# Narrow passes of a feature-major fp32 block: weight tiles that start at other bytes, and one ring slot read backwards

## The chip, the cores and the metric

One core of a Trainium2 chip runs the whole kernel. The metric is the device time of one execution in microseconds, as a median over several executions; lower is better.

## What is computed

The reference is one residual block over 256 tokens of width 2048, all in float32:

```python
h = rms_norm(x, ln_pre_mix)
proj = h @ w_in                                   # 2048 -> 7680 columns: u, v, q, k, v, two gates
y_a = gmlp_branch(u, v_sg, ...) @ w_a_out
y_b = swa_branch(q, k, v, rel_bias, sinks) @ w_b_out
mix = (gate_a * y_a + gate_b * y_b) @ w_o
x = x + rms_norm(mix, ln_post_mix)
h2 = rms_norm(x, ln_pre_ffn)
x = x + rms_norm(conv_ffn(h2, w_up, conv_w, w_down), ln_post_ffn)   # w_up: 2048 -> 16384, w_down: 8192 -> 2048
```

Each weight matrix is read once, and each product has only 256 rows, one per token.

## The kernel before

**Split numbers.** Every float32 operand of a large product is split into a high part (rounded to the type that TensorE takes at full rate) and a low part (the rest). A product is then three products: high by high, high by low, low by high. ScalarE rounds the high part of the weights (`w_hi`, line 453), VectorE subtracts it to get the low part (`w_lo`, line 861).

**Two ways to multiply.** In the token-major stages (the first projection, `w_o`, `w_down`) the weights are the moving operand: 128x512 passes at lines 1634, 1584, 1777 and 1597. In the feature-major stages the weights are the stationary operand, so that a result stands with its features on the partitions. These stages are q/k/v, u, the gates, `w_a_out`/`w_b_out` (called Y here) and `w_up`. A pass there loads a 128x128 tile of weights and streams activations from `actT`, which holds for each of 16 k-tiles 256 columns of high parts and then 256 of low parts:

- a **wide pass** (`by_hi`, line 1493) loads a tile of `w_hi` and streams all 512 columns, high and low activations;
- a **narrow pass** (`by_lo`, line 1497) loads a tile of `w_lo` and streams the 256 columns of high activations.

**Ring slots.** The weights of a stage come in halves of 1024 columns, numbered h = 0 to 7 in each turn. Half h stands in slot h % 4 of `w_hi` and of `w_lo`. A half gives 8 wide and 8 narrow passes, each with its own 128x128 tile, 512 bytes per partition. `w_hi` slots lie 4096 bytes apart, `w_lo` slots 4608 bytes, `actT` k-tiles 2048 bytes; in the built program the starts of all three are equal modulo 512 bytes. In `w_lo` the data of the feature-major stages begin 8 bytes behind the slot's start:

```python
w_lo_padded = sb("w_lo", [P, RING, HALF + P], F32R)
w_lo = w_lo_padded[:, :, 0:HALF]
w_lo_shifted = [w_lo_padded[:, slot, 2:2 + HALF] for slot in range(RING)]
```

`w_lo_shifted` is written by `split` of VectorE and read by `by_lo`; all other stages use `w_lo`, which begins at the slot's start. Among these is `half_a` (lines 1508 and 1513), which runs the first turn of `w_up`: the same wide and narrow passes, with the narrow ones from `w_lo`.

**The order on TensorE.** `group_turn` runs one turn of 8 halves as four `pair_a`: the pair (0, 1) wide and then narrow, the pair (2, 3) narrow and then wide (`lo_first`), and the same for (4, 5) and (6, 7). So TensorE sees runs of 32 narrow passes (slots 0, 1, 2, 3, 8 passes each) between runs of 32 wide ones (slots 2, 3, 0, 1). In the four turns of Y no pair is `lo_first`, and the runs have 16 passes (slots 0, 1 or 2, 3). 48 turns of 64 wide and 64 narrow passes make 3072 of each. Between some pairs small products of the attention stand.

The loads of weights from memory, ScalarE's rounding and VectorE's subtraction run ahead of TensorE by the ring's four slots; they wait for `half_used`, which TensorE raises once per half.

Of the kernel before, what the change touches and what calls it, by code (L numbers as in the profile page):

```python
# [12 lines left out]
P = 128  # L13
S = 256
# [21 lines left out]
HALF = UNIT // 2  # L36
RAW = 4
RING = 4
# [24 lines left out]
def block_program(nc, x, x_t, pre_gains, w_in, ln_v_g, ln_v_b, w_spatial, b_spatial, rel_bias, sinks, w_a_out, w_b_out,  # L63
# [10 lines left out]
    with ExitStack() as ctx:  # L74
        def sb(name, shape, dt=F32):
            return ctx.enter_context(nc.sbuf_tensor(name, shape, dt))
# [6 lines left out]
        w_hi = sb("w_hi", [P, RING, HALF], F32R)  # L83
        w_lo_padded = sb("w_lo", [P, RING, HALF + P], F32R)
        w_lo = w_lo_padded[:, :, 0:HALF]
        w_lo_shifted = [w_lo_padded[:, slot, 2:2 + HALF] for slot in range(RING)]
        actT = sb("actT", [P, KD, 2, S], F32R)
        xs = sb("xs", [P, RING, 2, S], F32R)
        a_parts = sb("a_parts", [P, 2, 3 * P], F32R)
# [90 lines left out]
        ps = ctx.enter_context(nc.psum_tensor("ps", [P, 8, 512], F32))  # L180
# [1310 lines left out]
        def _(pe):  # L1491
# [2 lines left out]
                                 actT[:, k, :, :].rearrange("p a s -> p (a s)"), start=start, stop=stop)  # L1494

            def by_lo(h, at, k, c, bank, start, stop):
                return pe.matmul(ps[:, bank + c, 0:S], w_lo_shifted[h % RING][:, at:at + P], actT[:, k, 0, :],  # L1497
                                 start=start, stop=stop)

            def half_a(m, h, k0, bank, rows_before):  # L1500

# [39 lines left out]
            def pair_a(m, h0, k0, k_first, k_last, bank, lo_first=False, branch_lo=False):  # L1541
# [14 lines left out]
                def run_lo(signal):  # L1556
                    for h in (h0, h0 + 1):
                        pe.wait_ge(lo_ready, 8 * m + (h + 1))
                        if branch_lo and lo_first:
                            pe.wait_ge(br_lo, h + 1)  # L1560
                        for i in range(4):
                            k = k0 + (h - h0) * 4 + i
                            for c in range(2):
                                ins = by_lo(h, i * GC + c * P, k, c, bank, lo_first and k == k_first,
                                            not lo_first and k == k_last)
                        if signal:
                            ins.then_inc(half_used, 1)
# [356 lines left out]
```

## Time and profile before

| | before |
|---|---|
| median of 3 runs | 1583.93 us (1583.9 to 1583.99) |
| the profiled execution: its own time | 1583.59 us |
| its span, first to last instruction | 1581.8 us |
| TensorE matmul busy | 1572.7 us (99%) |
| TensorE weight load busy | 1360.7 us (86%) |
| VectorE busy | 1260.6 us (80%) |
| ScalarE busy | 827.8 us (52%) |
| wide passes, line 1493 | 3072, 717.6 us |
| narrow passes, line 1497 | 3072, 377.9 us |

Matmuls overlap in the profile, because each one's end is modelled with the time through the array. The length of one (390 ns for a wide pass) is therefore not what it costs: the distance from one start to the next is. A row of the timeline that merges n passes tells it as (its length minus one pass's length) / (n - 1). A row of the grouped view gives nearly the same as busy time over count.

### The profile page before, as it was taken

The numbers are of one execution on the slowest core, as the hardware profiler recorded it, in microseconds if no ns is written. First come the engines' busy times: TensorE is split into PE (matmuls) and PEld (weight loads), VectorE is DVE, ScalarE is ACT, GpSimd is POOL, SyncE is SP. The second block draws the span as 40 slices with busy tenths as digits, with TensorE's granted clock in tenths as the row PEclk, the third lists the DMA queues.
The fourth block names the chain that finished last, engine by engine and source line by source line (L and its number), as shares of the span: only waits on it lengthen the run. The fifth ranks groups of instructions, "written<-read, shape, count | busy, mean of one in ns | idle before, by whom it ended". The sixth has DMA issues, their size and how long they took to land.

```text
span 1581.8 us, 24342 instructions
## 1 busy us (share of the span) xinstructions
PE 1572.7 (99%) x8652; PEld 1360.7 (86%) x8652; DVE 1260.6 (80%) x1836; ACT 827.8 (52%) x1124; POOL 1.9 (0%) x12
## 2 busy tenths in 40 slices
PE   9999999999999999999999999999999999999998
PEld 8888888888888888888888888888888888888886
DVE  6566677677797788777787777877778899989998
ACT  7544544456565654444444444444444575766664
POOL 0000000000000000000000000000000000000000
PEclk9999999999999999999999999999999999999999
DMA  9885455556566465556655666665655555555562
GB/s 371 272 232 189 160 186 168 178 160 209 191 241 218 152 210 188 187 186 203 190 189 187 186 201 191 190 187 186 200 191 191 209 208 206 201 204 195 186 213 107
DMA packets 234946, 313.15 MB, mean 198 GB/s; under 512 B 5360, under 2 KB 209808, under 8 KB 234000
## 3 DMA queue, kind: packets, MB, share of 16 engines
q1 hardware_dynamic: 231056, 306.44, 58.8%
q10 hardware_dynamic: 3840, 6.05, 1.5%
q8 instruction: 32, 0.52, 0.1%
q14 instruction: 18, 0.15, 0.0%
HBM read 309.58 MB, written 2.88 MB: 198 GB/s over the span
## 4 chain that ended last, share of the span: by engine, by line
PE 96%; DVE 4%; issue 0%; ACT 0%; DVEq 0%
PE ps L1493 44%; PE ps L1497 23%; PE ps L1584 15%; PE ps L1777 6%; PE ps L1634 3%; PE ps L1597 1%; DVE actT L1188 1%; DVE w_lo L1188 1%; PE ps L1508 1%; PE ps L1513 0%; DVE arena L1176 0%; PE ps L1723 0%; PE ps L1704 0%; PE ps L1656 0%; PE ps L1716 0%
## 5 line engine op out<-in xcount | busy, mean ns | idle before, releaser
L1493 PE MATMUL ps<-actT,w_hi 128*128 128x512 f32 x3072 | 717.6, 390 | 0.0
L453 ACT ACTIVATE w_hi<-raw 128x1024 fp32r<-128x1024 f32 x420 | 433.1, 1055 | 504.6 <-PE ps L1493 253.7
L861 DVE TENSOR_TENSOR w_lo<-raw,w_hi 128x1024 fp32r<-128x1024 f32 x422 | 506.4, 1224 | 232.3 <-ACT w_hi L453 230.1
L1493 PEld LDWEIGHTS ps<-actT,w_hi 128*128 128x128 f32 x3072 | 568.9, 188 | 114.6 <-issue 0.2
L1497 PEld LDWEIGHTS ps<-actT,w_lo 128*128 128x128 f32 x3072 | 372.4, 188 | 10.3 <-issue 1.7
L1497 PE MATMUL ps<-actT,w_lo 128*128 128x256 f32 x3072 | 377.9, 279 | 0.0
L1584 PE MATMUL ps<-w_hi,xs 128*128 128x512 f32 x832 | 226.6, 389 | 0.0
L1584 PEld LDWEIGHTS ps<-w_hi,xs 128*128 128x128 f32 x832 | 156.1, 188 | 32.4
L1584 PE MATMUL ps<-w_lo,xs 128*128 128x512 f32 x416 | 128.1, 389 | 0.0
L1188 DVE TENSOR_TENSOR w_lo<-raw,w_hi 128x1024 fp32r<-128x1024 f32 x96 | 117.4, 1222 | 0.0
L1378 DVE SCALAR_TENSOR_TENSOR arena<-arena,convw 128x256 f32<-128x256 f32 x256 | 106.8, 480 | 0.0
L712 ACT ACTIVATE w_hi<-raw 128x1024 fp32r<-128x1024 f32 x96 | 100.5, 1046 | 0.0
L1584 PEld LDWEIGHTS ps<-w_lo,xs 128*128 128x128 f32 x416 | 78.1, 188 | 16.3
L1777 PE MATMUL ps<-actT 128*128 128x512 f32 x288 | 81.0, 389 | 0.1
L690 ACT ACTIVATE actT<-raw 128x1024 fp32r<-128x1024 f32 x24 | 25.4, 1060 | 99.0 <-PE ps L1777 99.0
L872 DVE TENSOR_TENSOR arena<-ps,arena 128x512 f32<-128x512 f32 (+1 forms) x106 | 72.6, 685 | 1.5 <-ACT arena L466 1.4
L1777 PE MATMUL ps<-actT,a_parts 128*128 128x512 f32 x216 | 64.7, 390 | 0.0
L1777 PEld LDWEIGHTS ps<-actT 128*128 128x128 f32 x288 | 54.0, 188 | 11.8 <-DVE actT L1188 0.6
L466 ACT ACTIVATE arena<-ps 128x512 f32<-128x512 f32 x106 | 61.4, 579 | 2.8 <-PE ps L1513 1.4
L1188 DVE TENSOR_TENSOR actT<-arena,actT 128x1024 fp32r<-128x1024 f32 (+2 forms) x52 | 59.8, 1161 | 0.0
L710 ACT ACTIVATE xs<-arena 128x256 fp32r<-128x256 f32 x96 | 38.8, 404 | 24.7 <-PE ps L1584 13.8
L1366 DVE TENSOR_TENSOR arena<-arena,rrow 128x512 f32<-128x512 f32 x64 | 44.3, 692 | 6.5
(181 smaller groups left out, 935.4 us busy)
## 6 DMA issues: line engine op xcount, KB each, us to landing
raw<-in_w_up_dram SPq DMA_DIRECT2D x128, 1024.0 KB, 5.7
raw<-in_w_down_dram SPq DMA_DIRECT2D x64, 1024.0 KB, 5.2
raw<-in_w_in_dram SPq DMA_DIRECT2D x58, 1024.0 KB, 5.2
raw<-in_w_o_dram SPq DMA_DIRECT2D x16, 1024.0 KB, 5.3
raw<-in_w_a_out_dram SPq DMA_DIRECT2D x8, 1024.0 KB, 5.3
raw<-in_w_b_out_dram SPq DMA_DIRECT2D x8, 1024.0 KB, 5.2
arena<-in_x_dram SPq DMA_DIRECT2D x1, 2048.0 KB, 16.7
arena<-in_x_dram ACTq DMA_DIRECT2D x2, 1024.0 KB, 6.3
```

The costliest lines, as they stand in the source:

```text
L453: act.activation(w_hi[:, h % RING, :], raw[:, h // 2, h % 2 * HALF:(h % 2 + 1) * HALF], ACT.Copy)\
L466: act.activation(lo_part, ps[:, bank:bank + 2, S:2 * S], ACT.Copy).then_inc(copied, 1)
L712: act.activation(w_hi[:, slot, :], raw[:, unit.slot, j * HALF:(j + 1) * HALF], ACT.Copy).then_inc(hi_ready, 1)
L861: dve.tensor_tensor(lo, raw[:, h // 2, h % 2 * HALF:(h % 2 + 1) * HALF], w_hi[:, h % RING, :].bitcast(F32), ALU.subtract).then_inc(lo_read ...
L872: dve.tensor_tensor(dst, ps[:, bank:bank + 2, 0:S], lo_part, ALU.add).then_inc(summed, 1)
L1188: return dve.tensor_tensor(lo, full, hi.bitcast(F32), ALU.subtract)
L1378: dve.scalar_tensor_tensor(out=dst[:, a, :], in0=src[:, a, i:i + S], scalar=w(i, a), in1=dst[:, a, :], op0=ALU.mult, op1=ALU.add).then_inc ...
L1493: return pe.matmul(ps[:, bank + c, :], w_hi[:, h % RING, at:at + P], actT[:, k, :, :].rearrange("p a s -> p (a s)"), start=start, stop=stop)
L1497: return pe.matmul(ps[:, bank + c, 0:S], w_lo_shifted[h % RING][:, at:at + P], actT[:, k, 0, :], start=start, stop=stop)
L1584: ins = pe.matmul(ps[:, bank + 2 * t + c, :], xpart[:, tokens], wpart[:, slot, c * 512:(c + 1) * 512], start=(first and xpart is x_hi and ...
L1634: ins = pe.matmul(ps[:, 4 + 2 * t + c, :], xpart[:, t * P:(t + 1) * P], wpart[:, slot, c * 512:(c + 1) * 512], start=(k == 0 and xpart is ...
L1777: ins = pe.matmul(ps[:, bank, :], x[x_part], y[y_part], start=(unit.first and alone and x_part + y_part == 0), stop=(unit.last and alone a ...
```

## The change

Three numbers and a direction change. The low parts of the feature-major stages begin 34, 50 and 18 floats (136, 200 and 72 bytes) behind the start of slots 0, 1 and 2; in slot 3 they stay at 2 floats (8 bytes). All four are the old 8 bytes plus a multiple of 64: plus 128, 192, 64 and 0. VectorE writes them there, and the narrow passes load their tiles from there. The narrow passes of slot 3 stream their 256 columns from the last to the first, and write their 256 results from the last to the first, so that each result stands where it stood. No instruction is added, removed or moved on any engine, and no wait changes.

```diff
         w_lo = w_lo_padded[:, :, 0:HALF]
-        w_lo_shifted = [w_lo_padded[:, slot, 2:2 + HALF] for slot in range(RING)]
+        LO_SHIFT = (34, 50, 18, 2)
+        w_lo_shifted = [w_lo_padded[:, slot, shift:shift + HALF] for slot, shift in enumerate(LO_SHIFT)]
+        BACKWARDS = 3
...
             def by_lo(h, at, k, c, bank, start, stop):
-                return pe.matmul(ps[:, bank + c, 0:S], w_lo_shifted[h % RING][:, at:at + P], actT[:, k, 0, :],
-                                 start=start, stop=stop)
+                step = -1 if h % RING == BACKWARDS else 1
+                return pe.matmul(ps[:, bank + c, 0:S][:, ::step], w_lo_shifted[h % RING][:, at:at + P],
+                                 actT[:, k, 0, ::step], start=start, stop=stop)
```

## Rows read from the trace of the kernel before

**Rows 1.** The page: busy time by engine, granted clock in 40 slices, chain that ended last.

```profile
PE 1572.7 (99%) x8652; PEld 1360.7 (86%) x8652; DVE 1260.6 (80%) x1836; ACT 827.8 (52%) x1124; POOL 1.9 (0%) x12
...
PEclk9999999999999999999999999999999999999999
...
PE 96%; DVE 4%; issue 0%; ACT 0%; DVEq 0%
PE ps L1493 44%; PE ps L1497 23%; PE ps L1584 15%; PE ps L1777 6%; PE ps L1634 3%; PE ps L1597 1%; DVE actT L1188 1%; DVE w_lo L1188 1%; PE ps L1508 1%; PE ps L1513 0%; DVE arena L1176 0%; PE ps L1723 0%; PE ps L1704 0%; PE ps L1656 0%; PE ps L1716 0%
```

**Rows 2.** Waits of TensorE: engine line waited for, us, times, longest.

```profile
PE ps L1656 <- DVE rrow L929: 1.2, 1, 1.2
PE ps L1823 <- DVE arena L1294: 0.5, 1, 0.5
PE ps L1525 <- DVE actT L918: 0.4, 1, 0.4
```

**Rows 3.** The page's groups: busy us, mean ns of one, idle before.

```profile
L1493 PE MATMUL ps<-actT,w_hi 128*128 128x512 f32 x3072 | 717.6, 390 | 0.0
...
L861 DVE TENSOR_TENSOR w_lo<-raw,w_hi 128x1024 fp32r<-128x1024 f32 x422 | 506.4, 1224 | 232.3 <-ACT w_hi L453 230.1
L1493 PEld LDWEIGHTS ps<-actT,w_hi 128*128 128x128 f32 x3072 | 568.9, 188 | 114.6 <-issue 0.2
L1497 PEld LDWEIGHTS ps<-actT,w_lo 128*128 128x128 f32 x3072 | 372.4, 188 | 10.3 <-issue 1.7
L1497 PE MATMUL ps<-actT,w_lo 128*128 128x256 f32 x3072 | 377.9, 279 | 0.0
...
L1188 DVE TENSOR_TENSOR w_lo<-raw,w_hi 128x1024 fp32r<-128x1024 f32 x96 | 117.4, 1222 | 0.0
```

**Rows 4.** Timeline of TensorE in two turns of w_up: start us, length us, line.

```profile
704.45 3.87 PE L1497 MATMUL ps<-actT,w_lo 128*128 128x256 f32 x32
708.15 7.44 PE L1493 MATMUL ps<-actT,w_hi 128*128 128x512 f32 x32
715.43 3.87 PE L1497 MATMUL ps<-actT,w_lo 128*128 128x256 f32 x32
719.14 7.45 PE L1493 MATMUL ps<-actT,w_hi 128*128 128x512 f32 x32
```

**Rows 5.** Timeline of TensorE in the first turn of w_up.

```profile
540.64 1.11 PE L1513 MATMUL ps<-actT,w_lo 128*128 128x256 f32 x8
541.59 1.04 PE L1831 MATMUL ps<-ident,arena 128*128 128x128 f32 x8
...
544.31 1.12 PE L1513 MATMUL ps<-actT,w_lo 128*128 128x256 f32 x8
545.26 2.00 PE L1508 MATMUL ps<-actT,w_hi 128*128 128x512 f32 x8
```

**Rows 6.** Two lines of code: duration ns min/median/max, first and last start.

```profile
L1513 PE MATMUL ps<-actT,w_lo x48: 277/283/283, 540.6 to 557.2; 128*128 128x256 f32 x48
...
L1831 PE MATMUL ps<-ident,arena x24: 270/272/273, 535.1 to 548.8; 128*128 128x128 f32 x24
```

**Rows 7.** Timeline of TensorE, five short windows: start and middle of runs.

```profile
540.88 0.88 PE L1513 MATMUL ps<-actT,w_lo 128*128 128x256 f32 x6
...
704.45 0.75 PE L1497 MATMUL ps<-actT,w_lo 128*128 128x256 f32 x5
...
704.80 1.43 PE L1497 MATMUL ps<-actT,w_lo 128*128 128x256 f32 x11
...
708.15 1.55 PE L1493 MATMUL ps<-actT,w_hi 128*128 128x512 f32 x6
...
711.81 2.43 PE L1493 MATMUL ps<-actT,w_hi 128*128 128x512 f32 x10
```

**Rows 8.** Windows, line 1497 alone: busy of PE, of PEld, clock, DMA.

```profile
49.00:337.00 288.00, 99.02 (x784) 95.69 (x784) 1.00 0.62 192
337.00:426.00 89.00, 30.93 (x244) 30.50 (x245) 1.00 0.57 181
...
557.00:1239.00 682.00, 240.32 (x1984) 238.80 (x1984) 1.00 0.61 191
```

**Rows 9.** Windows, all engines: PE, PEld, DVE, ACT, POOL busy.

```profile
557.00:1239.00 682.00, 682.00 (x3974) 602.81 (x3974) 533.42 (x788) 305.55 (x347) 0.00 (x0) 1.00 0.61 191
```

## The prediction

> **What bounds the kernel now.** I read the page first. TensorE is busy for 99% of the span at a granted clock of nine tenths or more in every slice, and the chain that ended last runs through it for 96% [rows 1]. In that chain the wide passes of line 1493 hold 44% and the narrow passes of line 1497 hold 23%. The waits of TensorE come to 2.1 us in three places, none of them at either line [rows 2]. So no engine keeps TensorE waiting in the feature-major stages; what counts there is how fast one pass follows another. VectorE, the busiest of the others, works 533 us of the 682 us of w_up [rows 9]. It could follow a TensorE that is some per cent faster.
>
> The second reading is the distance between starts. The timeline shows a run of 32 narrow passes from 704.45 to 708.15, which is 3.70 / 32 = 115.6 ns each, and then 32 wide ones to 715.43, 227.5 ns each [rows 4]. Columns alone don't give these numbers: a wide pass has twice the columns of a narrow one, so 227.5 - 115.6 = 111.9 ns would be the price of 256 columns, and the narrow pass costs 3.7 ns more than that. Per pass, a tile of 128x128 weights is loaded beside the stream of the pass before, and the load itself is shown as 188 ns long [rows 3].
>
> The third reading is the one on which the forecast turns. The first turn of w_up runs the same narrow pass, with the same two operands, but with tiles that begin at the slot's start (line 1513). Six of them in the middle of a run take (0.88 - 0.283) / 5 = 119.4 ns each [rows 6, 7]. Eleven of line 1497, whose tiles begin 8 bytes further, take (1.43 - 0.279) / 10 = 115.1 ns each [rows 3, 7]. So where a tile begins, relative to the columns that are streamed, moves a narrow pass by 4.3 ns. Over 3072 passes that is 13 us.
>
> The Trainium skill says otherwise (SBUF — State Buffer, Who interferes with whom): TensorE has a read port for the stream and another for the weights, and never waits for anyone. By that rule a start address is free, the two rows should read alike, and this change would be worth 0 us. The trace disagrees, by those 4.3 ns; the rule comes back below as a rival.
>
> **The change part by part.**
>
> *The writes of VectorE.* It subtracts into the slots at another byte. Between the old 8 bytes (line 861, 1224 ns) and none (line 1188, 1222 ns) there is no difference to speak of [rows 3]. Cost 0, covered besides by VectorE's idle time; were the cover gone, 2 ns x 422 would be under 1 us.
>
> *Slots 0, 1 and 2: 2304 of the 3072 narrow passes.* No row has a tile that begins 64, 128 or 192 bytes behind the place where the stream begins, so I bound it. Below: a 128x128 pass from the identity (line 1831) streams half the columns of a narrow one and loads a tile of the same size; eight follow each other at (1.04 - 0.272) / 7 = 109.7 ns [rows 5, 6]. That they do not run at half the narrow pass's distance tells that the load of the tile sets them, and a narrow pass can't do better than its load. From 115.1 to 109.7 is 5.4 ns, times 2304 is 12.4 us gained. Above: the price without any offset, 119.4 ns, which is 4.3 x 2304 = 9.9 us lost.
> Which value? The rows have only one step away from equal starts, and it was a gain. They don't say whether the gain came from those 8 bytes inside a small unit, which all four slots keep, or from distance as such, which grows in three slots. I take half of the way that is left to the load's price: 2.7 ns x 2304 = 6.2 us gained. This is a choice between ends that lie on both sides; it is the weakest number here.
>
> *Changes of place inside a run.* A run doesn't reach its pace at once. The first five narrow passes after wide ones take (0.75 - 0.279) / 4 = 117.8 ns, against 115.1 in the middle; six wide ones after narrow ones take (1.55 - 0.39) / 5 = 232 ns against (2.43 - 0.39) / 9 = 226.7 ns in the middle [rows 3, 7]. TensorE settles again whenever the relation of tile and stream changes. Today slots 0 to 3 have one relation, so a run of 32 settles once. With four relations it settles at three more places, 2 runs in each of 44 turns, and at one more place in each of the 16 runs of 16 in Y: 264 + 16 = 280 places. The price of one is 4 passes x 2.7 ns = 11 ns, so 3.0 us lost. Below, it is 0, if the slots don't differ; above, 8 passes at 2.7 ns, 6.0 us.
>
> *Slot 3 backwards: 768 passes.* No row has a stream that goes backwards, in or out. Both streams keep their bytes; only the sense in which the activations run against the tile's load turns round. Below, the load's price again: 5.4 x 768 = 4.1 us gained. Above, a stream that goes at half its pace would cost a narrow pass what a wide one costs, 227.5 - 115.6 = 112 ns more, and 768 x 112 = 86 us. These ends are far apart; the nearest row is the forward pass itself, which reads the same operands in the same places, and I take 0.
>
> *Sum.* -6.2 + 3.0 + 0 = -3.2 us. The profiled execution took 1583.59 us, so 1580.4; the median of before lies 0.3 us higher, so **1580.7 us** after. All of it is on the path: 784, 244 and 1984 narrow passes lie in the three stretches [rows 8], and TensorE has no slack there.
>
> **The rivals.**
>
> *Nothing moves.* If only the place inside a unit of 64 bytes counts, the 8 bytes that all slots keep are all there is; the three added distances are multiples of 64 and change nothing, and direction may be as idle. For it: the 8 bytes had their effect although they are a small part of a 512-byte tile, and within a run the slots 0, 1, 2 and 3 begin 4608 bytes apart and yet run evenly. Against it: wide passes settle over several passes, so the relation of the two streams over longer distances counts too. The skill's rule above leads to the same place for another reason, and the trace has gone against that reason. Time: 1583.9 us.
>
> *The relation gets worse.* The old offset may be a good place, and others worse. A narrow pass then sits at the price of an unsettled or an aligned one. At 117.8 ns for slots 0 to 2 it is 2.7 x 2304 = 6.2 us lost, with the 3.0 us of settling 9.2, so 1593 us; at 119.4 ns 9.9 + 3.0 = 12.9, so 1597. For it: the unsettled paces of the rows are all slower than the settled ones, narrow and wide, and 8 passes per slot leave little time to settle. Against it: a settled pace was reached from every start that the trace has. Smaller losses belong here too: with the settling's 3.0 us already lost, 0.2 us more make the result slower by over 0.2%.
>
> *Backwards is dear.* Here one thing alone ends on the slower side: the pass of slot 3 pays for reading or writing from last to first. Its place is every fourth stay in a ring slot, 768 passes. It cancels the gain of 3.2 us from 4.2 ns per pass and makes the kernel slower by over 0.2% from 8.4 ns; at half pace the sum is +83 us, so 1667. For it: nothing in this kernel goes that way, so no row vouches for it. Against it: neighbours stay neighbours, and the bytes touched are the same. The skill (Advanced Engine Details and Errata, PSUM Cachelines) asks that every two consecutive elements of an output lie together, in lines of 8 bytes, and says that matmuls slow down otherwise. A backward output keeps its pairs, so by the letter of the rule it is free; no run so far shows it.
>
> **How the numbers follow.** 0.2% of this time is 3.2 us, about what a measurement of this kernel can tell from no change. The forecast case, a gain in the moved slots that outweighs the settling, is the likeliest at 0.45: of its outcomes some stay under 0.2% and most, up to the bound of 12.4 + 4.1 = 16.5 us, are beyond it. Nothing moves: 0.20. A worse relation: 0.28. Backwards dear: 0.07. From these come faster by over 0.2% 0.40 (the forecast case less the part that is too small), same 0.27 (nothing moves, and the small ends of the two cases beside it), slower 0.33. The range must leave out no more than 2 in 10: below, 1571 us takes in all but the last 4 us of the bound; above, 1595 takes in the worse relation up to the unsettled price and a little of the way to the aligned one, and leaves the rest of it and the dear backward pass outside. For the likeliest case alone the range is 1570 to 1583.
>
> **What would show it.** In the profile after, the runs of 32 narrow passes have four stays of 8, and windows over each give a pace per slot. The forecast wants slots 0 to 2 at about 112.4 ns once settled, a slower first pass or two after each change of slot, slot 3 near 115, and wide passes at 226.7 as before. Nothing moved would show all four at 115. A worse relation would show paces from 117 to 120 in slots 0 to 2. A dear backward pass stands out in slot 3 alone. Line 861 should stay at 1224 ns, and the waits of TensorE at 2.1 us. What would make it all wrong: that the pace of wide passes changes because the load of `w_hi` tiles follows the last narrow passes in another relation, which no term here holds; or that a distance of 64 bytes and more has an effect of another size than the two rows of lines 1497 and 1513 span.

## The result and the profile after

| | before | after |
|---|---|---|
| median | 1583.96 us (4 runs) | 1591.26 us (4 runs, 1590.91 to 1591.54) |
| ratio | | 1.0046, 95% interval 1.0034 to 1.0059 |
| profiled execution, span | 1581.8 us | 1589.7 us |

The change made the kernel 7.3 us slower. The prediction said 1580.7 us, faster, with a range from 1571 to 1595. The measured time lies inside the range, but the kernel moved the other way.

The page of the kernel after, busy time by engine, the chain, and the groups that answer to [rows 3] (by_hi stands at line 1495 now, by_lo at 1500, VectorE's subtraction at 863):

```profile
PE 1580.4 (99%) x8652; PEld 1368.7 (86%) x8652; DVE 1260.6 (79%) x1836; ACT 828.0 (52%) x1124; POOL 1.9 (0%) x12
...
PE ps L1495 44%; PE ps L1500 23%; PE ps L1587 15%; PE ps L1780 6%; PE ps L1637 2%; PE ps L1600 1%; DVE actT L1190 1%; DVE w_lo L1190 1%; PE ps L1511 1%; DMA raw<-in_w_in_dram 1%; PE ps L1516 0%; DVE arena L1178 0%; PE ps L1726 0%; PE ps L1707 0%; PE ps L1719 0%
...
L1495 PE MATMUL ps<-actT,w_hi 128*128 128x512 f32 x3072 | 716.6, 390 | 0.0
...
L863 DVE TENSOR_TENSOR w_lo<-raw,w_hi 128x1024 fp32r<-128x1024 f32 x422 | 506.3, 1223 | 239.9 <-ACT w_hi L455 237.7
...
L1500 PEld LDWEIGHTS ps<-actT,w_lo 128*128 128x128 f32 x3072 | 380.2, 188 | 10.8 <-issue 1.7
L1500 PE MATMUL ps<-actT,w_lo 128*128 128x256 f32 x3072 | 386.1, 282 | 0.0
...
L1587 PE MATMUL ps<-w_hi,xs 128*128 128x512 f32 x832 | 226.6, 389 | 0.0
```

The loss stands in one row. The narrow passes went from 377.9 to 386.1 us, 8.2 us more, and the wide ones from 717.6 to 716.6, 1.0 us less; together 7.2 us. VectorE's writes to the new places cost what they did (506.3 against 506.4 us), and the token-major passes kept their 226.6 us; of before the page has:

```profile
L1584 PE MATMUL ps<-w_hi,xs 128*128 128x512 f32 x832 | 226.6, 389 | 0.0
```

The waits of TensorE (engine line waited for, us, times, longest) are those of [rows 2] and one of 0.2 us:

```profile
PE ps L1659 <- DVE rrow L931: 1.2, 1, 1.2
PE ps L1826 <- DVE arena L1296: 0.5, 1, 0.5
PE ps L1528 <- DVE actT L920: 0.4, 1, 0.4
PE ps L1637 <- ACT w_hi L455: 0.2, 1, 0.2
```

So TensorE waits 0.2 us more than it did, and the other 7 us are not waits; its passes follow each other more slowly. The timeline of TensorE shows where. One run of 32 narrow passes in w_up, the run of wide ones behind it, and then windows that take 7 passes of each stay of 8, in slots 0, 1, 2 and 3, and the first ten wide passes:

```profile
708.16 3.96 PE L1500 MATMUL ps<-actT,w_lo 128*128 128x256 f32 x32
711.96 7.43 PE L1495 MATMUL ps<-actT,w_hi 128*128 128x512 f32 x32
...
708.28 0.99 PE L1500 MATMUL ps<-actT,w_lo 128*128 128x256 f32 x7
...
709.23 0.98 PE L1500 MATMUL ps<-actT,w_lo 128*128 128x256 f32 x7
...
710.17 1.00 PE L1500 MATMUL ps<-actT,w_lo 128*128 128x256 f32 x7
...
711.12 1.00 PE L1500 MATMUL ps<-actT,w_lo 128*128 128x256 f32 x7
...
711.96 2.44 PE L1495 MATMUL ps<-actT,w_hi 128*128 128x512 f32 x10
```

The run takes 711.96 - 708.16 = 3.80 us where [rows 4] had 3.70. Slot by slot, (length - 0.28) / 6 gives 118, 117, 120 and 120 ns; no stay is at the 115.1 ns of [rows 7].

A hundredth of a microsecond is coarse for that. The turns of w_up repeat so exactly that the starts can be averaged over 28 of them, which gives each distance to a tenth of a ns. In thirteen of the seventeen kernels below the distances then come out as whole multiples of 0.833 ns, the "units" of the expectations; in all_1, all_10, enter_34_stay_50 and act_8 many don't. This table is worked out from the traces in that way: mean distance from start to start in ns in each stay of 8 passes, and the time of a turn (two runs of 32 narrow and two of 32 wide passes). The places are bytes from the slot's start.

```
kernel             places of slots 0-3      narrow, slot 0    1      2      3    wide, first 8   turn, us
before             8 8 8 8                         116.7  115.6  115.4  115.4          230.0     21.973
after              136 200 72 8, 3 backwards       117.8  117.8  119.9  119.7          227.9     22.147
shifts_only        136 200 72 8                    117.8  117.8  119.9  117.3          227.8     22.107
back_only          8 8 8 8, 3 backwards            116.7  115.6  115.4  118.6          232.2     22.080
all_34             136, all slots                  117.8  117.8  118.2  117.8          230.6     22.133
all_18             72, all slots                   118.6  118.1  118.2  118.3          230.1     22.147
all_50             200, all slots                  118.8  120.0  120.0  119.8          229.8     22.227
all_0              0, all slots                    119.1  120.0  120.0  120.0          230.1     22.227
all_back           8, all slots, all backwards     119.2  119.9  120.0  120.0          228.2     22.200
enter_34_stay_50   136 200 200 200                 117.8  117.6  116.7  116.7          231.3     22.107
all_66             264, all slots                  116.7  115.6  115.4  115.4          230.0     21.973
all_1              4, all slots                    117.8  118.3  118.3  117.8          230.0     22.133
all_4              16, all slots                   118.3  118.3  118.3  118.3          232.0     22.173
all_6              24, all slots                   121.1  121.2  121.5  121.9          227.9     22.307
all_10             40, all slots                   118.3  119.2  119.2  119.0          230.1     22.173
hi_8               8, w_hi at 8 too                116.7  115.6  115.4  115.6          230.5     22.180
act_8              8, actT at 8 too                119.9  119.6  120.7  119.5          232.2     22.547
```

In all rows but the last two the wide passes settle at 226.7 ns. In hi_8 the two narrow runs of a turn differ in their first stay, 116.7 and 117.6 ns; the row shows one. The table holds for w_up. Of the 121 narrow runs of the kernel 71 have 32 passes, 62 of them in w_up; the other 50, in the stages before it, have 16.

### The profile page after: what moved, and what is told of

Same layout as the page of the kernel before. It is cut to its first block, busy times and chain, and to the rows that moved or that the text cites. A ratio compares the mean times of both kernels' runs of the same rounds, so it can differ in the third digit from the quotient of the medians.

```text
span 1589.7 us, 24342 instructions
## 1 busy us (share of the span) xinstructions
PE 1580.4 (99%) x8652; PEld 1368.7 (86%) x8652; DVE 1260.6 (79%) x1836; ACT 828.0 (52%) x1124; POOL 1.9 (0%) x12
## 4 chain that ended last, share of the span: by engine, by line
PE 95%; DVE 4%; DMA 1%; SPq 0%; issue 0%; ACT 0%; DVEq 0%
PE ps L1495 44%; PE ps L1500 23%; PE ps L1587 15%; PE ps L1780 6%; PE ps L1637 2%; PE ps L1600 1%; DVE actT L1190 1%; DVE w_lo L1190 1%; PE ps L1511 1%; DMA raw<-in_w_in_dram 1%; PE ps L1516 0%; DVE arena L1178 0%; PE ps L1726 0%; PE ps L1707 0%; PE ps L1719 0%
## 5 line engine op out<-in xcount | busy, mean ns | idle before, releaser
L1495 PE MATMUL ps<-actT,w_hi 128*128 128x512 f32 x3072 | 716.6, 390 | 0.0
L863 DVE TENSOR_TENSOR w_lo<-raw,w_hi 128x1024 fp32r<-128x1024 f32 x422 | 506.3, 1223 | 239.9 <-ACT w_hi L455 237.7
L1500 PEld LDWEIGHTS ps<-actT,w_lo 128*128 128x128 f32 x3072 | 380.2, 188 | 10.8 <-issue 1.7
L1500 PE MATMUL ps<-actT,w_lo 128*128 128x256 f32 x3072 | 386.1, 282 | 0.0
L1587 PE MATMUL ps<-w_hi,xs 128*128 128x512 f32 x832 | 226.6, 389 | 0.0
L1587 PE MATMUL ps<-w_lo,xs 128*128 128x512 f32 x416 | 128.1, 389 | 0.0
```

Of the source, the lines that this page charges most:

```text
L863: dve.tensor_tensor(lo, raw[:, h // 2, h % 2 * HALF:(h % 2 + 1) * HALF], w_hi[:, h % RING, :].bitcast(F32), ALU.subtract).then_inc(lo_read ...
L1495: return pe.matmul(ps[:, bank + c, :], w_hi[:, h % RING, at:at + P], actT[:, k, :, :].rearrange("p a s -> p (a s)"), start=start, stop=stop)
L1500: return pe.matmul(ps[:, bank + c, 0:S][:, ::step], w_lo_shifted[h % RING][:, at:at + P], actT[:, k, 0, ::step], start=start, stop=stop)
L1587: ins = pe.matmul(ps[:, bank + 2 * t + c, :], xpart[:, tokens], wpart[:, slot, c * 512:(c + 1) * 512], start=(first and xpart is x_hi and ...
```

## The experiments

### The two parts by themselves

From here on the diffs are against the kernel after; the step is -1 where `h % RING in BACKWARDS`. First the places without the direction:

```diff
         LO_SHIFT = (34, 50, 18, 2)
-        BACKWARDS = 3
+        BACKWARDS = ()
```

> The three moved slots as in the change, slot 3 forwards again. Every theory must give back what the trace after shows of slot 3: its stay of 8 narrow passes takes 0.957 us there against 0.923 before. Theory 1 (each offset has a pace of its own): slots 0, 1, 2 stay at about 0.943, 0.943 and 0.959 us per stay, slot 3 returns to 0.923 to 0.93 us; the kernel takes 1588 to 1590 us. Theory 2 (every change of offset costs a settling, whatever the offset): slot 3 still follows a slot with another offset, so its stay remains above 0.94 us; 1590 to 1591 us. Theory 3 (the backward pass is the only loss): 1584 us.

Measured: 1589.15 us, before beside it 1583.80, ratio 1.0033 (1.0021 to 1.0046). So the three places alone lose 5.4 us. The stays of slots 0 to 2 are those of the kernel after, to a tenth of a ns. Slot 3 came back to 117.3 ns, not to 115.4: it follows a slot with another place and pays 1.9 ns x 8 = 15 ns for that. Theories 1 and 2 each have a part of it. Theory 3, by which the backward pass was the only loss, falls.

Then the direction without the places:

```diff
-        LO_SHIFT = (34, 50, 18, 2)
-        BACKWARDS = 3
+        LO_SHIFT = (2, 2, 2, 2)
+        BACKWARDS = (3,)
```

> All four slots at 8 bytes as before, slot 3 backwards. If the backward pass costs by itself, slot 3 takes 0.95 to 0.96 us per stay and slots 0 to 2 stay at 0.923 to 0.934; a part of the 0.034 us per stay comes back in the wide passes that follow, since those after the change settle in 2 passes and not in 5; 1585.5 to 1587.5 us. If it lost only because of its neighbours' offsets, 1584 us. If direction is all of the loss, 1591 us.

Measured: 1587.94 us, ratio 1.0026 (1.0017 to 1.0036). The backward slot alone loses 4.1 us, more than the 1585.5 to 1587.5 that I had for it. The timeline of TensorE, 7 passes of slot 3 and the first ten wide passes behind them:

```profile
709.24 1.00 PE L1500 MATMUL ps<-actT,w_lo 128*128 128x256 f32 x7
...
710.07 2.48 PE L1495 MATMUL ps<-actT,w_hi 128*128 128x512 f32 x10
```

The same window of the wide passes in the kernel before:

```profile
708.15 2.46 PE L1493 MATMUL ps<-actT,w_hi 128*128 128x512 f32 x10
```

The passes themselves cost 118.6 against 115.4 ns, 3.2 x 8 = 26 ns per stay. The wide passes behind them then take (2.48 - 0.39) / 9 = 232.2 ns where (2.46 - 0.39) / 9 = 230.0 is the time of before, so in w_up they lose nearly as much again. In the kernel after, the same window gives (2.44 - 0.39) / 9 = 227.8, and shifts_only has the same in the table. So behind three moved slots the wide passes settle sooner, whichever way slot 3 goes. The grouped views of shifts_only (first two lines) and of back_only:

```profile
L1495 PE MATMUL ps<-actT,w_hi 128*128 128x512 f32 x3072 | 716.2, 390 | 0.0
L1500 PE MATMUL ps<-actT,w_lo 128*128 128x256 f32 x3072 | 384.5, 281 | 0.0
...
L1495 PE MATMUL ps<-actT,w_hi 128*128 128x512 f32 x3072 | 719.0, 391 | 0.0
L1500 PE MATMUL ps<-actT,w_lo 128*128 128x256 f32 x3072 | 380.5, 280 | 0.0
```

Over the whole kernel the backward slot alone costs 2.6 us in the narrow row and 1.4 in the wide one. 5.4 and 4.1 us together are more than the 7.3 us of the whole change for two reasons of about 1 us each. In the wide row, 1.4 us less and 1.4 us more would cancel, and the whole change has 1.0 us less. In the narrow row, 6.6 and 2.6 us would make 9.2, and the whole change has 8.2: slot 3 has a loss in either part alone, and the two don't add up.

### One place in all four slots

```diff
+        LO_SHIFT = (34,) * 4           # all_34; 18, 50, 0 likewise
+        BACKWARDS = ()
```

> All four slots at 136 bytes, all forwards, so no change of offset inside a run. Theory 1 (each offset has its pace): the pace of slot 0 after, 117.8 ns, holds in all four slots and never falls to 115.6; the kernel takes 1589 to 1592 us. Theory 2 (only changes of offset cost): after the first five passes of a run the pace is 115.6 ns, and the kernel takes 1584 us.

> All four slots at 72 bytes, all forwards. Theory 1 (each offset has its pace): 119.9 ns as in slot 2 after, or whatever it settles to with 32 passes at hand, but not 115.6; 1594 to 1598 us. Theory 2 (only changes of offset cost): 1584 us. A third outcome is possible: 72 bytes settles to a pace of its own only after more than 8 passes, so the stays of the second half of a run are faster than the first.

> All four slots at 0 bytes, forwards: tiles and stream begin at equal places modulo 512 bytes. Theory 1 (each offset has its pace) expects the pace of line 1513 of before, 120 ns, in all 3072 passes: 4.4 ns more than at 8 bytes, 1595 to 1597 us. If line 1513 is slow for another reason (runs of 8 only, other semaphores), about 1584 us.

> All four slots at 200 bytes, forwards. Slot 1 after showed 140 units of 0.833 ns (116.7 ns) in six passes in a row behind a slot at 136 bytes. Theory 1 (each offset has its pace): 116.7 ns holds through the run, 1586 to 1588 us. If slot 1 owed its pace to its neighbours, the pace is another, between 117.5 and 120 ns, and 1590 to 1596 us.

| | place, bytes | median, us | ratio to before (95%) |
|---|---|---|---|
| all_34 | 136 | 1590.79 | 1.0044 (1.0028 to 1.0060) |
| all_18 | 72 | 1591.74 | 1.0050 (1.0034 to 1.0066) |
| all_0 | 0 | 1595.05 | 1.0070 (1.0050 to 1.0090) |
| all_50 | 200 | 1594.32 | 1.0065 (1.0045 to 1.0086) |

With no change of place inside a run, none of them comes back to the time of before. Theory 2, by which only changes cost, falls: a place has a pace. At 136 bytes slot 0's 117.8 ns holds in all slots, as expected. At 0 bytes the narrow passes of the whole kernel take on the pace of line 1513, 120.0 ns, so that line's pace needs no other reason than its place. The timeline of TensorE in all_0, one run:

```profile
709.75 4.00 PE L1500 MATMUL ps<-actT,w_lo 128*128 128x256 f32 x32
713.58 7.44 PE L1495 MATMUL ps<-actT,w_hi 128*128 128x512 f32 x32
```

(4.00 - 0.283) / 31 = 119.9 ns. The loads of the narrow tiles are shown 192 ns long in this run, against 188 before. In all_50, at the same 120.0 ns, they are shown 189 ns long. So the length of the load doesn't tell the pace.

But two of the four went against the plain form of theory 1, and against the times that it gave. At 72 bytes the pace is 118.2 ns, not the 119.9 that slot 2 showed in the change. At 200 bytes it is 120.0 ns, not the 116.7 that slot 1 settled to in the change (six distances of 140 units in a row).

### Can one place have two paces?

```diff
+        LO_SHIFT = (34, 50, 50, 50)    # enter_34_stay_50
+        BACKWARDS = ()
```

> Slot 0 at 136 bytes, slots 1, 2 and 3 at 200 bytes, all forwards. At 200 bytes in all slots a narrow pass took 144 units of 0.833 ns; in slot 1 after, behind a slot at 136 bytes, 140 units, six times in a row. If one offset has more than one settled pace and the entry decides, slots 1 to 3 hold 140 units for up to 24 passes and the kernel takes 1588 to 1590 us. If the 140 of slot 1 was a passage on the way to 144, the later stays climb to 144 and the kernel takes 1591 to 1594 us.

Measured: 1590.30 us, ratio 1.0039 (1.0023 to 1.0055), which lies between the times of the two theories, 0.3 us above the first and 0.7 below the second. The pace decides. The timeline of TensorE, 15 passes of slots 2 and 3:

```profile
709.59 1.92 PE L1500 MATMUL ps<-actT,w_lo 128*128 128x256 f32 x15
```

and in all_50, the last 16 passes of a run, at the same place:

```profile
710.88 2.08 PE L1500 MATMUL ps<-actT,w_lo 128*128 128x256 f32 x16
```

(1.92 - 0.28) / 14 = 117 ns against (2.08 - 0.28) / 15 = 120 ns. The same 200 bytes, the same operands, the same engine work: entered from wide passes the run settles at 120.0 ns, entered by way of 8 passes at 136 bytes it settles at a mean of 116.7 and holds that for 23 passes to the run's end. So this place has two settled paces, and what came before decides which.

### Backwards in all four slots

```diff
+        LO_SHIFT = (2,) * 4            # all_back
+        BACKWARDS = (0, 1, 2, 3)
```

> All four slots at 8 bytes, every narrow pass backwards. Slot 3 alone backwards cost 31 units of 0.833 ns per stay of 8 passes against forwards, and the wide passes behind it took 22 to 33 more. If backwards has a pace of its own (142.5 units, 118.7 ns), the kernel takes 1592 to 1595 us. If what cost was the change of direction inside a run, the later stays return to 138 to 139 units and the kernel takes 1584 to 1587 us.

Measured: 1594.33 us, ratio 1.0065 (1.0045 to 1.0086). Backwards has a pace of its own at this place, 120.0 ns against the 115.6 of before, and it doesn't recover in the later stays. A stream at half its pace is excluded: 4.4 ns, not 112. Whether the cost comes from reading backwards, from writing backwards, or from the stream's first column lying 1020 bytes further on, no run here separates. Nor did any run go backwards at another place.

### Where the good place is, and what repeats

```diff
+        LO_SHIFT = (66,) * 4           # all_66; 1, 4, 6, 10 likewise
+        BACKWARDS = ()
```

> All four slots at 264 bytes, 8 plus 256, forwards. If the relation of tile and stream repeats after 256 bytes, the pace is that of 8 bytes, 115.6 ns, and the kernel takes 1584 us. If the place in the whole tile of 512 bytes counts, the pace is another one, between 117 and 120 ns as at 72, 136 and 200 bytes: 1590 to 1595 us.

> All four slots at 4 bytes, forwards. With a straddled small unit as the cause, 4 bytes gives a pace between those of 0 and 8 bytes or equal to that of 8: 115.6 to 120 ns, 1584 to 1595 us. Under 1583 us would show that 8 bytes was not the best place.

> All four slots at 16 bytes, forwards. If the gain of 8 bytes over 0 comes from a tile that straddles a small unit, a whole 16 bytes gives 0's pace back, 120 ns and 1595 us. If it comes from distance, 16 bytes is as good as 8 or better, 1580 to 1585 us.

> All four slots at 24 bytes, 8 plus 16, forwards. If only the place inside 16 bytes counted, 24 would be as 8: 1584 us; the runs at 72, 136 and 200 bytes speak against it. Else a pace between 140 and 144 units, 1589 to 1595 us. A pace under 138 units, below 1583 us, would be a better place than before's.

> All four slots at 40 bytes, 8 plus 32, forwards. With places of 72, 136 and 200 bytes at 142, 141.5 and 144 units, a smooth curve over the distance would give about 140 units, 1587 us; without one, anything from 138 to 144 units, 1583 to 1595 us. Below 1583 us would be a better place than before's.

| | place, bytes | median, us | ratio to before (95%) |
|---|---|---|---|
| all_66 | 264 | 1583.74 | 0.9999 (0.9988 to 1.0010) |
| all_1 | 4 | 1590.85 | 1.0044 (1.0024 to 1.0063) |
| all_4 | 16 | 1592.39 | 1.0052 (1.0029 to 1.0075) |
| all_6 | 24 | 1598.16 | 1.0090 (1.0060 to 1.0119) |
| all_10 | 40 | 1592.63 | 1.0054 (1.0032 to 1.0077) |

The timeline of TensorE in all_66, one run:

```profile
704.41 3.87 PE L1500 MATMUL ps<-actT,w_lo 128*128 128x256 f32 x32
708.11 7.45 PE L1495 MATMUL ps<-actT,w_hi 128*128 128x512 f32 x32
```

This is [rows 4] again, and in the averaged starts each of the 128 distances of a turn agrees with before to about a tenth of a unit. Moving a tile by 256 bytes does nothing, at this one place where it was tried; moving it by 64, 128 or 192 does. And all_6, one run:

```profile
710.93 4.05 PE L1500 MATMUL ps<-actT,w_lo 128*128 128x256 f32 x32
```

24 bytes give (4.05 - 0.285) / 31 = 121.5 ns, worse than no offset at all, although 24 is 8 plus 16. So neither the place within 16 bytes nor the distance orders the paces: 0, 4, 8, 16, 24 and 40 bytes stand at 120.0, 118.3, 115.4, 118.3, 121.5 and 119.2 ns. 16 bytes met neither of its two expectations, and 24 bytes lies above its range. Among the nine places tried, and 264 as 8, 8 is the only fast one, and no version here beats the kernel before.

### Tile or stream?

```diff
-        w_hi = sb("w_hi", [P, RING, HALF], F32R)
+        w_hi_padded = sb("w_hi", [P, RING, HALF + P], F32R)                       # hi_8
+        w_hi = w_hi_padded[:, :, 2:2 + HALF]
...
-        actT = sb("actT", [P, KD, 2, S], F32R)
+        actT_padded = sb("actT", [P, KD * 2 * S + P], F32R)                       # act_8
+        actT = actT_padded[:, 2:2 + KD * 2 * S].rearrange("p (k a s) -> p k a s", k=KD, a=2)
```

Both start from the kernel before, with its 8 bytes in `w_lo`, and these diffs are against it. The padding also sets the slots of `w_hi` 4608 instead of 4096 bytes apart and moves what lies behind; all this is in multiples of 512 bytes, and no run has the padding without the 8 bytes.

> The kernel before, with the high parts begun 8 bytes behind the slot's start too, in all stages. If what the 8 bytes do to a narrow pass comes from the relation of a tile's place and the stream's, the wide passes gain as the narrow ones did, from 272 units (226.7 ns) to about 267 (222 ns): 3072 x 4.4 ns = 13.6 us, 1570 to 1573 us, and possibly the passes of lines 1584, 1777 and 1634 move as well, where w_hi is the stream. If wide passes are set by something else, 1584 us; if 8 bytes cost the stream, slower.

Measured: 1601.61 us, ratio 1.0111 (1.0094 to 1.0128), the largest miss of the study. The grouped view of hi_8 (busy us, mean ns of one, idle before):

```profile
L1494 PE MATMUL ps<-actT,w_hi 128*128 128x512 f32 x3072 | 726.2, 393 | 0.0
...
L1498 PE MATMUL ps<-actT,w_lo 128*128 128x256 f32 x3072 | 378.1, 279 | 0.0
...
L1585 PE MATMUL ps<-w_hi,xs 128*128 128x512 f32 x832 | 232.0, 395 | 0.0
L1585 PE MATMUL ps<-w_lo,xs 128*128 128x512 f32 x416 | 130.0, 393 | 0.0
```

The narrow passes stayed (378.1 against 377.9 us). The wide ones, whose tile moved by the 8 bytes that help a narrow pass, became slower, 717.6 to 726.2 us. So did the token-major ones, where the same 8 bytes moved the stream and not the tile, 226.6 to 232.0. The `w_lo` passes that stand between these went from 128.1 to 130.0 us with both of their operands where they were, modulo 512 bytes.

> The kernel before with the activations too begun 8 bytes further, so that narrow passes have tile and stream at equal places again, both 8 bytes from the usual ones. If the relation of the two decides, narrow passes take the 144 units (120 ns) of all slots at 0 bytes, and the wide ones, whose tile now begins 8 bytes ahead of the stream, leave 272 units. If the tile's own place decides, narrow passes keep 138.67 units (115.6 ns) and wide ones 272, and the kernel takes 1584 us.

Measured: 1614.71 us, ratio 1.0194 (1.0164 to 1.0224). The grouped view of act_8:

```profile
L1496 PE MATMUL ps<-actT,w_hi 128*128 128x512 f32 x3072 | 732.1, 395 | 0.0
L1501 PE MATMUL ps<-actT,w_lo 128*128 128x256 f32 x3072 | 389.9, 283 | 0.0
...
L1781 PE MATMUL ps<-actT 128*128 128x512 f32 x288 | 82.9, 396 | 0.0
```

and two lines to compare, from all_0 and from before:

```profile
L1500 PE MATMUL ps<-actT,w_lo 128*128 128x256 f32 x3072 | 389.4, 283 | 0.0
...
L1777 PE MATMUL ps<-actT 128*128 128x512 f32 x288 | 81.0, 389 | 0.1
```

The tile of a narrow pass stands where it stood before, and the pass lost its 115.4 ns: the tile's own place doesn't decide alone. Its mean over a stay is 119.5 to 120.7 ns, that of equal places at 0 bytes (389.9 against 389.4 us in all_0), but the distances are not the even 144 units that I expected; they run from 139 to 149. The wide passes left 272 units for about 280.

That fits the relation of tile and stream, but doesn't prove it, for a stream that begins 8 bytes further may cost by itself. One case shows that the relation is not all. The 288 passes of line 1777 read both operands from `actT`, so in act_8 tile and stream moved together and their relation stayed. They took 82.9 us instead of 81.0; where two of them follow each other, 234.0 ns instead of 227.4. So the stream's own place, or that of both, counts too. A run with the stream at 8 and the tile at 16 bytes would tell how much of the narrow pass's 4 ns belongs to the relation; it was not made.

## Why the prediction was wrong

**What bounds the kernel** was right: the passes of TensorE and their distance, no wait beyond 0.2 us, nothing of VectorE; the loss is all in line 1500's row.

**The step that failed** is the value for slots 0, 1 and 2: "I take half of the way that is left to the load's price: 2.7 ns x 2304 = 6.2 us gained." It took the one step that the rows had, from 0 to 8 bytes, as the beginning of a direction. In its place the three slots lost. In w_up they lose 1.1, 2.2 and 4.5 ns per pass (the table). Over the whole kernel, the distances of the traces summed by slot, they lose 0.9, 1.6 and 2.8 us, together 5.2 us, with the settling at each change in it; slot 2 lost less before w_up, where 25 of its 34 stays begin a run. The places alone, run as shifts_only, cost 5.4 us. The runs with one place show why no direction was there: 8 and 264 bytes read alike, the paces go up and down between them, and 8 bytes was the one fast place of those tried. Why 8 bytes is fast stays open.

The upper bound of that term, 119.4 ns from line 1513, held for slots 0 and 1; slot 2 stood 0.5 ns above it. The lower bound was not sound. The passes of line 1831 follow each other at 109.7 ns, but their loads are shown 141 ns long and those of the narrow passes 188, so theirs is not the same load, and in no run did narrow passes settle under 115 ns. The 119.4 ns was read over five distances from a length rounded to 0.01 us; the starts themselves give 118.4 there and 120.0 in the five other runs of line 1513. The middle of a run at 8 bytes is 115.6, not 115.1. The difference is then 4.4 ns, so the forecast's 4.3 was right, in part by luck.

**Settling** was right in kind. Slot 3 forwards behind a slot with another place paid 15 ns where I had 11. The count was off: 71 runs of 32 and 50 of 16 have 3 x 71 + 50 = 263 changes of place inside a run, not 280. What it missed is that the entry can also put a run at another pace: slot 1 settled at 116.7 ns behind slot 0, where the same place takes 120.0 behind wide passes. Slot 2 took 119.9 ns in its 8 passes, where alone it takes 118.2.

**Slot 3 backwards** I took at 0; by itself it lost 4.1 us. The row that I called nearest, the forward pass, was the nearest in operands; that turning the stream round changes its relation to the load is an argument and not shown. 1.4 us of the loss are not in the backward passes but in the wide ones behind them, for which the sum had no term. The prediction named that gap as a way to be wrong. In the kernel after, the term has the other sign: the first wide passes take 227.9 instead of 230.0 ns, and the wide row fell by 1.0 us. Slot 3 itself lost 3.1 us there, by the distances summed over its 768 passes.

**The rivals.** "The relation gets worse", with a chance of 0.28, is what happened: 9.2 us forecast there, 7.3 measured, with paces of 117.8 to 119.9 ns where it had 117.8 for slots 0 to 2. That the two times lie so near is in part luck: it had nothing for slot 3, which lost 3.1 us, and 9.2 us for slots 0 to 2, which lost 5.2. Nor does the range speak for the sum, since its upper end was set by this rival. "Nothing moves" failed on its unit: 72, 136 and 200 bytes don't read as 8, and 264 does. "Backwards is dear" is excluded at half pace, but its smaller form came true beside the worse relation: by itself the backward slot cost 4.1 us, more than the 3.2 us of the forecast gain.

**The page's rule.** The Trainium skill (SBUF — State Buffer, Who interferes with whom) gives TensorE two independent read ports and lets only the pair that VectorE and GpSimd share cause contention. What the prediction took from it, that a start address is free, had the trace against it before and has the kernels of the table against it now: some bytes of place in one operand move a narrow pass between 115.4 and 121.5 ns at a granted clock of 0.998 or more. The page says nothing of addresses, and no run here shows that the two ports wait for each other. That the load of the next tile disturbs the running stream was argued from the paces, and no run took the load away. Why one entry settles at 116.7 ns and another at 120.0 also stays open.

## What to carry to other kernels

Where TensorE hardly waits, the start addresses of tile and stream can matter: here some tenths of a per cent for the tile of the narrow passes, and up to 1.9% when all of `actT` moved. It is not a knob with a direction, so measure each place, and alone. A kernel that gives each ring slot another place measures neighbours and entries with it, and reads a slot's pace wrongly by some 3 ns. A place found for one kind of pass doesn't carry over to another: the 8 bytes that gain 4.4 ns on a narrow pass cost a wide one 4 ns.

## What the hardware showed that I had not expected

- In the like turns of w_up the distances between matmul starts are whole multiples of 0.833 ns in thirteen of seventeen kernels, and the patterns repeat: 115.0, 115.0, 116.7 ns at 8 bytes, a cycle of ten distances at 136 bytes.
- One place and one instruction stream had two settled paces, 116.7 and 120.0 ns, each held to the run's end.
- A stream that goes backwards, in and out, runs at nearly the forward pace: 120.0 against 115.6 ns for 256 columns.
- Moving `w_hi` by 8 bytes slowed 3072 wide passes by 8.6 us, 832 token-major ones by 5.4 us, and the 416 passes between these, whose own operands kept their places modulo 512 bytes, by 1.9 us.
- Moving tile and stream together by 8 bytes, in act_8, slowed passes of line 1777 from 227.4 to 234.0 ns.
